# Expert rows of a mixture layer: gathered as quarter rows and turned on VectorE, in place of whole rows turned on TensorE

## What is computed

```python
    def expert_block(args):
        tok_idx, g, e = args
        xb = xt[tok_idx]
        yb = swiglu(xb, w_gate_e[e], w_up_e[e], w_down_e[e])
        return yb * g[:, None].astype(yb.dtype)

    y_rows = lax.map(expert_block, (src_tok.reshape(n_blocks, EXPERT_BLOCK),
                                    row_gate.reshape(n_blocks, EXPERT_BLOCK),
                                    block_expert))
    routed = jnp.zeros_like(xt).at[src_tok].add(y_rows.reshape(rows, d))
```

## Time and profile before

| | |
|---|---|
| time, median of 3 runs | 1634.29 us |
| profiled execution, span from first to last instruction | 1628.9 us |
| what lies around the span (median less span; the profiled execution's whole time is not given) | 5.4 us |
| busy: TensorE, VectorE, ScalarE, GpSimd | 95%, 47%, 40%, 41% |
| moved by DMA | 366.18 MB, mean 225 GB/s |
| chain that ended last: TensorE's share of the span | 54% |

### The profile page before, as it was taken

The page is one execution under the profiler, slowest core; times in us unless marked ns, Lnnn a source line. Parts: engine busy times, 40 slices in busy tenths (PEclk is TensorE's granted clock), DMA queues, the critical chain, the costliest instruction groups (busy, mean ns, idle before and its releaser), DMA issues.

```text
span 1628.9 us, 30259 instructions
## 1 busy us (share of the span) xinstructions
PE 1553.9 (95%) x10204; PEld 1337.6 (82%) x10204; DVE 761.0 (47%) x1536; ACT 653.2 (40%) x1054; POOL 671.1 (41%) x825
## 2 busy tenths in 40 slices
PE   6999999999798999899999999999999999999991
PEld 5789989989644667789999999999999999999990
DVE  4333788788688774433333333333333333333333
ACT  6434545444433312034444444444444444444443
POOL 0422245063303222435555554555555555555541
PEclk9999999999999999999999999999999999999996
DMA  5389321211250021479999999999999999999976
GB/s 183 99 290 309 123 78 52 77 55 52 98 216 27 30 62 66 165 267 307 318 318 326 313 305 320 314 314 314 321 308 314 309 315 315 314 313 314 313 234 221
DMA packets 100744, 366.18 MB, mean 225 GB/s; under 512 B 22279, under 2 KB 32424, under 8 KB 79710
## 3 DMA queue, kind: packets, MB, share of 16 engines
q1 hardware_dynamic: 60622, 246.60, 41.9%
q0 software_dynamic: 40080, 119.05, 26.4%
HBM read 300.68 MB, written 73.91 MB: 230 GB/s over the span
## 4 chain that ended last, share of the span: by engine, by line
PE 54%; DMA 1%; issue 0%; ACT 0%; POOL 0%; DVE 0%; SPq 0%; POOLq 0%; ACTq 0%
PE gu L1761 35%; PE ype L1783 4%; PE yrest L1772 4%; PE ype L1784 4%; PE ype L1785 4%; PE xp L1740 3%; PE xp L1747 1%; DMA A<-acc_rows 1%; DMA acc_rows<-YE,sia 1%; POOL acc_rows L1674 0%; DVE A L1947 0%; SPq L1634 0%; ACT junkf L1897 0%; ACT XS L1840 0%; PE ype L1747 0%
## 5 line engine op out<-in xcount | busy, mean ns | idle before, releaser
L1761 PE MATMUL gu<-XS,place 128*128 128x160 f32 x4160 | 586.0, 299 | 0.4 <-ACT XS L1836 0.4
L1761 PEld LDWEIGHTS gu<-XS,place 128*128 128x128 f32 x4160 | 573.5, 190 | 5.7 <-ACT XS L1840 0.7
L1910 DVE TENSOR_TENSOR WL<-place,WH 128x2048 fp32r<-128x2048 f32 x65 | 149.3, 2297 | 315.0 <-ACT WH L1832 315.0
L1674 POOL DMA_INDIRECT acc_rows<-YF,sib x65 | 105.5, 1624 | 197.8 <-issue 155.4
L1845 ACT ACTIVATE SS<-gu 128x160 f32<-128x160 f32 x130 | 39.4, 303 | 362.7 <-PE gu L1761 362.7
L1915 DVE TENSOR_TENSOR SS<-SS,gu 128x160 f32<-128x160 f32 x130 | 41.3, 317 | 253.5 <-ACT SS L1845 253.5
L1660 POOL COPY gta<-tables 128x1 f32 (+1 forms) x65 | 140.6, 2163 | 0.0
L1855 ACT ACTIVATE YE<-ype,gta 128x512 f32<-128x512 f32 x130 | 89.5, 688 | 109.7 <-PE ype L1785 109.7
L1131 POOL DMA_INDIRECT slot_table<-pay,si x64 | 62.0, 968 | 172.4 <-DVEq L1440 159.6
L1832 ACT ACTIVATE WH<-place 128x2048 fp32r<-128x2048 f32 x65 | 123.5, 1900 | 0.7 <-issue 0.7
L1679 POOL DMA_INDIRECT acc_rows<-YE,sia x65 | 103.5, 1593 | 43.9 <-issue 23.5
(11 more groups left out here) (317 smaller groups left out, 2798.2 us busy)
## 6 DMA issues: line engine op xcount, KB each, us to landing
place<-in_w_gate_e SPq DMA_DIRECT2D x65, 1024.0 KB, 7.1
place<-in_w_up_e SPq DMA_DIRECT2D x65, 1024.0 KB, 9.9
place<-in_w_down_e SPq DMA_DIRECT2D x65, 1024.0 KB, 14.0
place<-in_w_in POOLq DMA_DIRECT2D x16, 512.0 KB, 7.0
late_parts<-wq_parts POOLq DMA_DIRECT2D x8, 1024.0 KB, 5.9
late_parts<-xn_parts POOLq DMA_DIRECT2D x8, 1024.0 KB, 6.1
wf_parts<-late_parts POOLq DMA_DIRECT2D x8, 1024.0 KB, 5.1
w_low<-late_parts POOLq DMA_DIRECT2D x8, 1024.0 KB, 5.1
```

The costliest lines, as they stand in the source:

```text
L1674: pool.indirect_dma_start(acc_q, bass.IndirectOffsetOnAxis(ap=si[q][1][:, :], axis=0), YF[q][:, :], None, compute_op=ALU.add, bounds_check ...
L1761: last = pe.matmul(gu[f][:, k, :], raw[:, t, f * P:f * P + P], XS[:, q, t, :], start=(t == 0), stop=(t == KT - 1))
L1910: tt(WL[q][:, :], WR[q][2][:, :], WH[q][:, :].bitcast(F32), ALU.subtract).then_inc(s_dlo, 1)
```

## The change

The normalised rows are written in plain order. The 160 slots of an item are five runs of 32 slots. For each run GpSimd gathers 128 quarter rows of 1 KB: partition 32 a + c gets quarter a of slot c's row. Five such gathers fill `XQ` (128 partitions x 1280 elements). One VectorE transposition in 32 by 32 blocks, with strided access patterns on its input, turns them into `XS`. TensorE's turns, ScalarE's copies, the two PSUM tiles and the parity tables are gone. The table of indices now has five columns an item (4 x token + quarter), and the additions of the rest use the fifth.

```diff
@@ phase_out_route, GpSimd: first item
-            pool.indirect_dma_start(K.slot[0], None, xn2_d, bass.IndirectOffsetOnAxis(ap=K.idx[0][:, 0:1], axis=0)) \
-                .then_inc(K.s_g[0], 16)
-            pool.indirect_dma_start(K.slot[2][:, 0:D // 2], None, xn2_d.rearrange("r (h n) -> (r h) n", h=2), bass.IndirectOffsetOnAxis(ap=K.rest[:, 0:1], axis=0)) \
-                .then_inc(K.s_gr, 16)
+            quarters_d = xn2_d.rearrange("r (b n) -> (r b) n", b=QUARTERS)
+            for s in range(RUNS):
+                pool.indirect_dma_start(K.XQ[0][:, s * DQ:(s + 1) * DQ], None, quarters_d,
+                                        bass.IndirectOffsetOnAxis(ap=K.quart[:, s:s + 1], axis=0)).then_inc(K.s_g[0], 16)
@@ phase_out_route, TensorE: turns of the normalised rows
-                rows = X2[j % 2].rearrange("p (t k) -> p t k", t=KT)
+                rows = X2[j % 2].rearrange("p (k t) -> p t k", t=KT)
@@ phase_out_route, VectorE: the normalised rows
-                by_k = [a.rearrange("p (k t) -> p k t", t=KT) for a in (H[j % NH], gffn[:, :])]
-                stt(X2[j % 2].rearrange("p (t k) -> p k t", t=KT), by_k[0], sh[:, TT + j:TT + j + 1], by_k[1], ALU.mult, ALU.mult) \
-                    .then_inc(s_x2, 1)
+                stt(X2[j % 2], H[j % NH], sh[:, TT + j:TT + j + 1], gffn[:, :], ALU.mult, ALU.mult).then_inc(s_x2, 1)
@@ phase_out_route, VectorE: the tables
+            by_run = K.quart.rearrange("p (n s) -> p s n", s=RUNS)
+            ts(by_run[:, 0:RUNS - 1, :], ms[1][:, :, 0:ITEMS], float(QUARTERS), quarter[:, 0:1], ALU.mult, ALU.add)
+            step(ts(by_run[:, RUNS - 1, :], op[0][:, 0:ITEMS], float(QUARTERS), quarter[:, 0:1], ALU.mult, ALU.add))
+            dve.sem_inc(s_ix, 1)
...
@@ phase_experts, GpSimd
             def gather(q, n):
-                pool.tensor_copy(gi[q][:, :], K.idx[0][:, bass.ds(n, 1)]).then_inc(s_gi, 1)
+                pool.tensor_copy(gi[q][:, :], K.quart[:, bass.ds(n * RUNS, RUNS)]).then_inc(s_gi, 1)
                 pool.wait_ge(s_gi, n - 1)
                 pool.sem_inc(turn["pool"], 1)
-                pool.indirect_dma_start(XG[q][:, :], None, xn2_d, bass.IndirectOffsetOnAxis(ap=gi[q][:, :], axis=0)) \
-                    .then_inc(s_g[q], 16)
-            def gather_rest(m):
...
+                gather_runs(q, [gi[q][:, s:s + 1] for s in range(RUNS)])
+            def gather_runs(q, index):
+                for s in range(RUNS):
+                    pool.indirect_dma_start(XQ[q][:, s * DQ:(s + 1) * DQ], None, quarters_d,
+                                            bass.IndirectOffsetOnAxis(ap=index[s], axis=0)).then_inc(s_g[q], 16)
...
                 if ahead >= 2:
-                    pool.wait_ge(s_g[q], i * 16 + 32)
+                    pool.wait_ge(s_g[q], i * LANDED + 2 * LANDED)
                     pool.sem_inc(turn["pool"], 1)
-                    pool.wait_ge(s_tm, n * 2 + 6)
+                    pool.wait_ge(s_xk, n + 3)
                     pool.sem_inc(turn["pool"], 1)
                     gather(q, n + 4)
-                    if q == 0:
...
-                        gather_rest(i + 2)
                 add_rows(n, q)
...
+            gather_runs(1, [K.quart[:, RUNS + s:RUNS + s + 1] for s in range(RUNS)])
             gates(0, 0)
...
+            for q in two:
+                pool.wait_ge(s_g[q], LANDED)
+                pool.wait_ge(s_xk, q + 1)
+                gather(q, 2 + q)
@@ phase_experts, TensorE
                 if ahead >= 1:
-                    pe.wait_ge(s_xk, n * 2 + 4)
-                    pe.wait_ge(s_rk, i * 2 + (2 * q + 2))
+                    pe.wait_ge(s_xk, n + 2)
                     gate_up(1 - q, n + 1, 0, i + (q + 1))
-                if ahead >= 2:
-                    pe.wait_ge(s_g[q], i * 16 + 32)
-                    turned(q)
-                if ahead >= 1:
                     gate_up(1 - q, n + 1, 1, None)
-                if ahead >= 2 and q == 0:
-                    pe.wait_ge(s_gr, i * 16 + 32)
-                    pe.wait_ge(s_xk, n * 2 + 6)
-                    rest_turned(xp[0])
                 down_rest(q, n)
@@ phase_experts, ScalarE
-                if ahead >= 2:
-                    keep(0, q, n + 2)
-                    keep(1, q, n + 2)
...
@@ phase_experts, VectorE
+            def turned(q, n, landed):
+                if n is not None:
+                    dve.wait_ge(s_gu, n * 2 - 2)
+                dve.wait_ge(s_g[q], landed)
+                dve.sem_inc(turn["dve"], 1)
+                nc.vector.transpose(XS[:, q, :, :].rearrange("p t (s j) -> p s t j", s=RUNS),
+                                    XQ[q].rearrange("p (s i t) -> p s t i", s=RUNS, t=KT)).then_inc(s_xk, 1)
...
                 n, o = i * 2 + q, 1 - q
+                if ahead >= 2:
+                    turned(q, n + 2, i * LANDED + 2 * LANDED)
                 low_down(q, n)
...
+            for q in two:
+                turned(q, None, LANDED)
             hidden(0, 0, 0)
             hidden(1, 0, 0)
```

More of the change, by code:

```diff
@@ L78, in setup @@
     K.ones = sb("ones", [P, P])
[L79 to L82, removed]
+    K.tab = sb("tables", [P, max((3 + RUNS) * ITEMS, 2 * HW)])
+    K.idx = K.tab[:, 0:ITEMS].bitcast(I32)
+    K.gate = [K.tab[:, (1 + k) * ITEMS:(2 + k) * ITEMS] for k in range(2)]
+    K.quart = K.tab[:, 3 * ITEMS:(3 + RUNS) * ITEMS].bitcast(I32)
     K.expert = sb("expert", [1, ITEMS], I32)
@@ L89, in setup @@
     slots = K.wi[:, :, :].rearrange("p t n -> p (t n)")
+    K.XQ = [slots[:, i * RUNS * DQ:(i + 1) * RUNS * DQ] for i in range(2)]
     K.slot = [slots[:, i * D:i * D + D] for i in range(4)]
@@ L1011, in phase_out_route @@
         pay = sb("pay", [P, TT, TOPK, 2])
[L1012 to L1016, removed]
+        before = K.place[:, 5 * KT * FF:5 * KT * FF + P]
+        sgs, hs = sb("sgs", [P, 2, P]), tail[:, KT * E_N + 128:KT * E_N + 128 + 2 * P].rearrange("p (f t) -> p f t", f=2)
+        quarter, lowi, rowc, pidx = (sb(n, [P, 1]) for n in ("quarter", "lowi", "rowc", "pidx"))
         rowi = sb("rowi", [ITEMS, 1], I32)
@@ L1021, in phase_out_route @@
         tbl = late[0:ITEMS, 0:2 * CAP].rearrange("i (c w) -> i c w", w=2)
[L1022 to L1026, removed]
+        tbx = late[0:ITEMS, 320:320 + RUNS * P].rearrange("i (s a c) -> i s a c", s=RUNS, c=CAP1)
+        tgx = late[0:ITEMS, 320 + RUNS * P:320 + (RUNS + 1) * P].rearrange("i (a c) -> i a c", c=CAP1)
+        cnt, ext, inc, le, zero = (late[:, 1152 + k * E_N:1152 + (k + 1) * E_N] for k in range(5))
+        tex, base, rw, exf = (late[:, 1536 + 16 * k:1536 + 16 * k + 1] for k in range(4))
+        pr, tj = late[0:1, 1600:1601], late[0:1, 1616:1648]
         ms = [ps(f"ms{i}", [P, HEADS, P]) for i in range(2)]
@@ L1280, in _ @@
             pe.wait_ge(s_ti, 16)
+            pe.wait_ge(s_tx, 1)
+            for s in range(RUNS):
+                out = ms[1][:, s, 0:ITEMS] if s < RUNS - 1 else op[0][:, 0:ITEMS]
+                last = pe.transpose(out, tbx[:, s, :, :].rearrange("i a c -> i (a c)"), K.ident[0:ITEMS, 0:ITEMS])
+            last.then_inc(s_tp, 1)
             for k in range(2):
                 pe.transpose(op[1][:, k * ITEMS:(k + 1) * ITEMS], tbl[:, 0:P, k], K.ident[0:ITEMS, 0:ITEMS])
[L1283 to L1288, removed]
+            pe.wait_ge(s_tx, 2)
+            pe.transpose(op[1][:, 2 * ITEMS:3 * ITEMS], tgx[:, :, :].rearrange("i a c -> i (a c)"),
+                         K.ident[0:ITEMS, 0:ITEMS]).then_inc(s_tp, 1)
             hidden_part(TT - 1, 2)
@@ L1587, in phase_experts @@
         outv = out.rearrange("b (j p) n -> p (b j) n", p=P)
-        turn = {e: sem(f"turn_{e}") for e in ("sp", "pool")}
+        turn = {e: sem(f"turn_{e}") for e in ("sp", "pool", "dve")}
         block = ctx.enter_context(nc.Block())
         LIMIT = ITEMS // 2 - 1
+        LANDED = 16 * RUNS
         def pairs(engine):
@@ L1663, in add_rows @@
             def add_rows(n, q):
-                for r in two:
-                    pool.tensor_copy(si[q][r][:, :], K.idx[r][:, bass.ds(n, 1)]).then_inc(s_si, 1)
+                pool.tensor_copy(si[q][0][:, :], K.idx[:, bass.ds(n, 1)]).then_inc(s_si, 1)
+                pool.tensor_copy(si[q][1][:, :], K.quart[:, bass.ds(n * RUNS + (RUNS - 1), 1)]).then_inc(s_si, 1)
                 if not isinstance(n, int) or n > 0:
@@ L1724, in _ @@
             for q in two:
-                pool.wait_ge(s_g[q], last * 16 + 32)
+                pool.wait_ge(s_g[q], last * LANDED + 2 * LANDED)
                 pool.sem_inc(turn["pool"], 1)
-            pool.wait_ge(s_gr, last * 16 + 32)
-            pool.sem_inc(turn["pool"], 1)
             pool.wait_ge(s_ad, last * 64 + 96)
@@ L1734, in _ @@
             pe.sem_inc(s_y, 3)
-            def turned(q):
-                rows = XG[q][:, :].rearrange("p (t k) -> p t k", t=KT)
-                for t in range(KT):
-                    last = pe.transpose(xp[t // 4][:, t % 4, :], rows[:, t, :], K.ident[:, :])
-                    if t % 4 == 3:
```

(11 more changed lines are left out.)

96 lines of the change are left out of this document (20 added, 76 removed).

## The result

The changed kernel takes 1637.01 us (median of 20 runs, 1631.21 to 1644.04) against 1632.92 us for the kernel before on the same chips (20 runs, 1629.98 to 1634.79). The ratio is 1.0024, 95% interval 1.0013 to 1.0035: slower by a quarter of a per cent, where 1622 us and "faster" were forecast. The time lies inside the range of 1575 to 1668 us, the sign is wrong. The profiled execution took 1641.21 us, span 1638.8 us (before: 1628.9 us). It lies 4.2 us above its kernel's median. That is why the two spans differ by 9.9 us and the medians by 4.1.

The account below looks back on a forecast made before the run. TensorE bound the loop before; GpSimd's issues were to bound it after. A late start of 6.5 us plus 64 x (13.38 - 13.67) gave -12 us, so 1634.3 - 12 = 1622 us, range 1575 to 1668.

Parts of the forecast that it names:

- What bounds the loop: Expert loop: GpSimd, issuing five gathers an item, sets the pace with a 13.38 us cycle, above TensorE's 12.69.
- What TensorE has left: Expert loop: without its turns of expert rows, 1.09 us an item, TensorE keeps 12.69 us of work an item.
- The first rival: Expert loop: TensorE keeps the pace if the stall falls on few small copies only; 1569 us, chance 0.14.
- The stall by WL: Expert loop: VectorE's subtraction WL holds up GpSimd once an item, costing 1.65 us, between 1.01 and 2.29.
- Index copy to first gather: GpSimd's cycle in the loop: from the index copy's start to the first gather's start, 1.02 us.
- four pitches: GpSimd's cycle in the loop: four more gathers at a pitch of 1.28 us between back-to-back issues, 5.12 us.
- YF to YE: GpSimd's cycle in the loop: from the addition of rests YF to the addition YE, start to start, 1.96 us.
- the base: Expert loop: GpSimd's steps summed start to start, if it waits for nobody, 11.73 us an item before the stall.
- The cycle: Expert loop: GpSimd's time from one YF to the next, 11.73 + 1.65 = 13.38 us, for 64 cycles, against 13.67 before.
- The start: Start of the loop: five gathers an item delay the first YF to 730.5 us from 724.05, 6.5 us late.
- Routing stage and transposition: Contiguous store in routing: 0, ends 7 us gain or loss; VectorE's transposition in the loop: 1.43 us or 2.53, hidden.
- DMA's pace: Expert loop: DMA engines, 0.97 busy, keep the pace; cycle 13.4 to 13.9 us, middle about 1640 us, chance 0.14.

Follow-up runs that it names:

- plain store: Kernel before with only the routing stage's edit: VectorE stores normalised rows contiguously, TensorE's turns read them at a stride of eight elements; 1631.35 us, ratio 0.999.
- small rows: Changed kernel with the same five gathers an item, each of 128 rows of 64 bytes instead of 1 KB; 1642.49 us, ratio 1.007 to the kernel before.
- the kernel with both edits: Changed kernel with WL computed in four instructions and the next gathers' index copy moved ahead of YF; 1571.83 us, ratio 0.9621 to the kernel before.

## Why the prediction was wrong

The mechanism was right, and two terms of the sum were too small. The forecast was a span of 1628.9 - 12 = 1616.9 us; the measured one is 1638.8, 21.9 us more. (Between medians it is 15.0 us, 1637.01 against 1622; the profiled execution is one of the slower ones. The steps below are the profile's.) By steps:

**What bounds the loop: right.** GpSimd does, by its issues and not its bytes. Shown from both sides: two issues instead of five give 1566.65 us, four more in the kernel before give +55 us, a sixteenth of the bytes gives nothing, and with all bytes and issues in place the loop goes at TensorE's pace once GpSimd's sequence is shorter.

**What TensorE has left: right.** 12.69 us forecast, 12.65 and 12.64 in the two kernels where it is the bound. The first rival's 1569 us is what they take (1571.83 and 1566.65); its condition, that the stall falls on a few copies only, was not met by the change itself.

**The stall by WL: right.** 1.65 us was taken between 1.01 and 2.29; it is 1.58 an item, and cutting WL in pieces takes most of it away. Every long gather is one that starts inside WL: after 740 us there are 61 of them in the changed kernel, and they take 1.86 to 3.05 us. The 244 others take 0.94 to 1.03 us, and among these are 65 that lie wholly inside a transposition, like the one at 1007.11 inside 1006.94 to 1009.44. The Trainium skill ("SBUF — State Buffer", section "Who interferes with whom") says that a VectorE instruction with at most one SBUF input, outside the 2-port modes, does not contend with GpSimd; the 65 gathers agree. For an instruction with two SBUF inputs the same section of the Trainium skill infers that descriptor generation is not held. The 61 indirect DMAs are held. They also read their indices from SBUF, which that section has such an instruction contend with, so it stays open which of the two waits; what the prediction drew from it, that the stall would fall on copies alone, does not hold in either case.

**Index copy to first gather: wrong, and the largest miss.** The prediction took 1.02 us from 1032.57 to 1033.59. There the index copy took 0.18 us, because WL's stall on the gate copy had kept it clear of YE. In the changed kernel the three copies start while YE's issue is still running (1003.96, inside 1002.95 to 1004.53), take 0.76 us each, and the gather, which waits for the last, leaves 1.62 us after that one's start on average. The step sizes came from turns in which GpSimd had been held up elsewhere; a base without waiting needed them from turns without. With the other steps as forecast or a little under (four pitches 5.03 us for 5.12, YF to YE 1.93 for 1.96), the base is 12.2 us instead of 11.73. Moving the copy out of YE's way gave 40 us (1637 to 1597; in the profiles 61 x 0.75 = 46 us of cycle), more than this 0.6 us an item explains (61 x 0.6 = 37 us), because the gather then waits for no copy at all: the step from gtb to the first gather fell by 1.08 us, of which 0.33 were given back in other steps.

**The cycle.** 13.38 us forecast. Measured 13.81 for 61 cycles, and 9.84 for the last three, which issue no gathers; the prediction multiplied all 64 alike. 61 x 0.43 = 26.2 us more, less 3 x 3.54 = 10.6: 15.6 us of the 21.9.

**The start: wrong by 5.8 us** (first YF 736.31, forecast 730.5). The prediction let item 1's gathers leave at 699.34 as before; they left at 704.32. 4.1 us of these 5.0 were there at the first expert gather (691.58 against 687.46), the other 0.9 came between it and item 1's (12.7 us instead of 11.9); 0.8 us more came later. Without the lower clock near 660 us the first gather leaves between 687.46 and 688.14 (before, its kernel with the plain store, small rows), with it between 689.3 and 691.6 (the seven others, the before kernel with more issues among them). The kernel with small rows has the changed kernel's routing stage and is 3.4 us earlier, so that much of the 4.1 us is not a cost of the edited lines. That it comes from the clock is argued, not shown. Whether the change makes that clock more frequent stays open: it showed in six of seven profiles of kernels with the change and in one of three without. What does belong to the change is that the first gate and up products wait for five gathers and a transposition (706.27 us against 700.76; 4.1 of these 5.5 us were there at the first gather).

**Routing stage and transposition.** The store fell from 2.02 us to 1.28, and the edit alone moved the time by -2 us (interval -3.1 to -0.2): the 0 was right within that. The transposition takes 2.51 us, the upper end and not the 1.43 chosen; hidden in the loop, as said.

**DMA's pace: wrong as a rival.** Its 1640 us lies 3 us from the result by chance; its mechanism is refuted twice, by the small rows and by the kernel with both edits, which moves the same pieces at 342 GB/s.

With the two terms and the last three cycles right the sum would have been -12 + 61 x 0.43 - 10.6 + 5.8 = +9.4 us, against 9.9 between the spans. The break-even cycle was 13.57 us; the range of the stall alone (12.74 to 14.02) held the measured 13.81, and a chance of 0.51 for faster was drawn from a middle that left out 0.43 us.

## What to carry to other kernels

Count an engine's issues before its bytes: taking work off the busiest engine paid here (62 us) only once the engine that got three and a half more issues an item had been relieved. When a cycle is summed from steps, take each step from a turn in which the neighbours stand as they will stand, since a copy of 0.2 us took 0.76 beside the issue in front of it. Where one engine's long instruction holds another engine, cut it into pieces; and move the small copy whose semaphore the next issue needs. Here that gave 38 and 40 us each alone, 65 us together.

## What the runs showed of the hardware that was not expected

- An issue of an indirect DMA of 128 rows has a median of 0.99 us for rows of 1 KB and of 64 bytes alike, at a pitch of 1.25 to 1.28 us when one follows another.
- A GpSimd copy that starts beside the issue of an indirect addition takes 0.76 us instead of 0.2.
- One subtraction of 128 x 2048 with two SBUF inputs (2.25 us) made every gather that started inside it last 1.86 to 3.05 us; as four of 128 x 512 (2.49 us in sum), at most 1.49.
- A 32 by 32 block transposition of 128 x 1280 float32 takes 1.51 us from contiguous rows and 2.50 us at a stride of eight elements.
- A busy share of the DMA engines of 0.97 at 314 GB/s left room: other kernels reached 342 GB/s at a share of 1.01 to 1.02.
